# An encoder trunk in split fp32: FFN chunks and renewed residual turned by VectorE blocks and a bounce through HBM

## The reference

```
for layer in (0, 1):
    h = rms_norm(x, mixer_norm_w[layer])
    mixed = mixer(h) @ w_out          # layer 0: sliding-window attention and a gMLP gate; layer 1: stick-breaking attention
    x = x + mixed
    h = rms_norm(x, ffn_norm_w[layer])
    x = x + (silu(h @ w_gate) * (h @ w_up)) @ w_down    # hidden width 5632
```

## Time and profile before

| | |
|---|---|
| median of 3 runs | 2147.93 us (2147.77 to 2148.04) |
| the profiled execution | 2147.97 us, of which 2146.2 us is the span from first to last instruction |
| PE busy | 2136.4 us (100%) |
| DVE busy | 1196.3 us (56%) |
| ACT busy | 987.8 us (46%) |
| POOL busy | 8.8 us |
| DMA | 398.66 MB, 186 GB/s mean; the weights' queue took 55.7% of the 16 engines |

### The profile page before, as it was taken

The page is one execution under the profiler, slowest core; times in us unless marked ns, Lnnn a source line. Parts: engine busy times, 40 slices in busy tenths (PEclk is TensorE's granted clock), DMA queues, the critical chain, the costliest instruction groups (busy, mean ns, idle before and its releaser), DMA issues.

```text
span 2146.2 us, 26146 instructions
## 1 busy us (share of the span) xinstructions
PE 2136.4 (100%) x9708; PEld 1766.4 (82%) x9708; DVE 1196.3 (56%) x1314; ACT 987.8 (46%) x1150; POOL 8.8 (0%) x19
## 2 busy tenths in 40 slices
PE   9999999999999999999999999999999999999999
PEld 8777888888888888888888888888888888888887
DVE  6777555555555554555565566555555455554554
ACT  6466554443344434445455445554443444434443
POOL 1000000000000000000000000000000000000000
PEclk9999999999999999999999999999999999999999
DMA  9544565555556555545645554555555655556544
GB/s 327 189 138 150 183 196 189 183 196 185 196 188 194 183 192 195 194 158 189 200 160 159 174 176 157 178 194 196 178 193 195 196 179 194 191 190 191 192 157 157
DMA packets 199171, 398.66 MB, mean 186 GB/s; under 512 B 6640, under 2 KB 6656, under 8 KB 198848
## 3 DMA queue, kind: packets, MB, share of 16 engines
q1 hardware_dynamic: 197728, 392.72, 55.7%
q0 software_dynamic: 960, 2.90, 0.4%
q10 hardware_dynamic: 416, 2.13, 0.3%
HBM read 395.62 MB, written 2.10 MB: 185 GB/s over the span
## 4 chain that ended last, share of the span: by engine, by line
PE 98%; DVE 1%; ACT 1%; issue 0%; DMA 0%; DVEq 0%; SPq 0%
PE acc L980 31%; PE acc L982 31%; PE acc L981 31%; PE turn L996 2%; PE turn L1066 1%; PE turn L1116 0%; DVE w_lo L638 0%; PE zb L1091 0%; PE zb L1051 0%; ACT w_hi L434 0%; DMA raw<-in_w_in 0%; PE turn L1034 0%; PE turn L1117 0%; PE zb L1092 0%; ACT att L542 0%
## 5 line engine op out<-in xcount | busy, mean ns | idle before, releaser
L638 DVE TENSOR_TENSOR w_lo<-raw,w_hi 128x1024 fp32r<-128x1024 f32 (+1 forms) x760 | 905.2, 1201 | 647.2 <-ACT w_hi L434 645.5
L434 ACT ACTIVATE w_hi<-raw 128x1024 fp32r<-128x1024 f32 (+1 forms) x760 | 790.8, 1042 | 923.3 <-PE acc L982 920.4
L980 PE MATMUL acc<-w_hi,xT_hi 128*128 128x512 f32 x2016 | 793.3, 393 | 2.1 <-DVE w_lo L638 1.7
L982 PE MATMUL acc<-w_hi,xT_lo 128*128 128x512 f32 x2016 | 785.3, 390 | 0.0
L981 PE MATMUL acc<-w_lo,xT_hi 128*128 128x512 f32 x2016 | 785.0, 389 | 0.0
L980 PEld LDWEIGHTS acc<-w_hi,xT_hi 128*128 128x128 f32 x2016 | 378.7, 188 | 82.7 <-issue 6.0
L982 PEld LDWEIGHTS acc<-w_hi,xT_lo 128*128 128x128 f32 x2016 | 378.5, 188 | 79.0
L981 PEld LDWEIGHTS acc<-w_lo,xT_hi 128*128 128x128 f32 x2016 | 378.8, 188 | 78.2 <-issue 1.7
L980 PE MATMUL acc<-w_hi,m_hi 128*128 128x512 f32 x960 | 376.2, 392 | 1.8 <-DVE x_sb L725 0.9
L982 PE MATMUL acc<-w_hi,m_lo 128*128 128x512 f32 x960 | 373.8, 389 | 0.0
L981 PE MATMUL acc<-w_lo,m_hi 128*128 128x512 f32 x960 | 373.7, 389 | 0.0
(11 more groups left out here) (143 smaller groups left out, 547.2 us busy)
## 6 DMA issues: line engine op xcount, KB each, us to landing
raw<-in_w_gate SPq DMA_DIRECT2D x88, 1024.0 KB, 5.1
raw<-in_w_up SPq DMA_DIRECT2D x88, 1024.0 KB, 5.1
raw<-in_w_down SPq DMA_DIRECT2D x80, 1024.0 KB, 5.1
raw<-in_w_qkv SPq DMA_DIRECT2D x48, 1024.0 KB, 5.1
raw<-in_w_out SPq DMA_DIRECT2D x32, 1024.0 KB, 5.1
raw<-in_w_in SPq DMA_DIRECT2D x26, 1024.0 KB, 5.2
raw<-in_w_down SPq DMA_DIRECT2D x16, 512.0 KB, 3.7
raw<-in_w_in SPq DMA_DIRECT2D x4, 512.0 KB, 6.5
```

The source lines that it names most:

```text
L434: nc.scalar.activation(w_hi[:, s % RING, 0:nk, :], raw[:, u % RING, k:k + nk, :], ACTF.Copy).then_inc(hi_ready, 1)
L638: nc.vector.tensor_tensor(w_lo[:, s % RING, 0:nk, :], raw[:, (s // 2) % RING, k:k + nk, :], f32(w_hi[:, s % RING, 0:nk, :]), ALU.subtract) ...
L980: nc.tensor.matmul(dst, h, wh, start=q == 0 and k == 0, stop=False)
L982: ins = nc.tensor.matmul(dst, l, wh, start=False, stop=q == ph.per_chunk - 1 and k == nk - 1)
```

## The change

The eight TensorE transposes of each FFN chunk and of each renewed residual chunk go. In their place:

- DVE, right behind the last accumulator reading, transposes 32x32 blocks of the chunk into `folded` (`fold`, two instructions of 128x512).
- POOL writes `folded` (512 KB) to an HBM scratch `blocks` with one DMA, waits for it, and reads it back with four DMAs, one for each 32 partitions (128 KB each, runs of 512 bytes), into `spread` (`bounce`).
- ACT and DVE take from `spread` in place of `turn`, with the pieces of 32 positions put in order by their access patterns (`by_tile`), and at t = slots + 4 in place of slots + 1.
- PE waits for `fold_lo` in place of `dve_took`.

The turns of the layer's mixers (`in`, `qkv`) stay on PE. `qT` moves in the layout of SBUF, to give room to `folded` and `spread`. The diff's core:

```diff
+            def bounce(ph, i):
+                F = ph.fold(i)
+                pool.wait_ge(fold_done, F + 1)
+                pool.dma_start(blocks.rearrange("t p n -> p t n"), folded[:, :, :]).then_inc(fold_out, 16)
+                pool.wait_ge(fold_out, 16 * F + 16)
+                for b in range(QUARTERS):
+                    pool.dma_start(spread[b * BLK:(b + 1) * BLK, :, :, :].rearrange("j t a r -> j (t a) r"),
+                                   blocks[:, :, b * P:(b + 1) * P].rearrange("t (a j) r -> j (t a) r", a=QUARTERS)).then_inc(fold_landed, 16)
...
+            def fold_take_hi(ph, i, dst, src, scale=None):
+                act.wait_ge(fold_landed, 16 * QUARTERS * (ph.fold(i) + 1))
...
+                ins.then_inc(fold_hi, 1)
...
-                if t == ph.slots + 1:
-                    take_hi(ph.turn(i), [m_hi[:, bass.ds(4 * i, 4), :]], [turn[:, :].rearrange("p (k t) -> p k t", k=4)])
+                if t == ph.slots + 4:
+                    fold_take_hi(ph, i, [by_tile(m_hi[:, bass.ds(4 * i, 4), :])], [spread_tiles])
...
+            def fold(ph, i, src):
+                F = ph.fold(i)
+                dve.wait_ge(fold_out, 16 * F)
+                for tt in range(TT):
+                    ins = nc.vector.transpose(folded[:, tt, :].rearrange("p (b k t) -> p b k t", b=QUARTERS, k=GRP),
+                                              src[:, tt, :].rearrange("p (k b j) -> p b k j", k=GRP, b=QUARTERS))
+                ins.then_inc(fold_done, 1)
...
-                if t == 17:
-                    hv = m_hi[:, bass.ds(4 * i, 4), :]
-                    take_lo(ph.turn(i), [m_lo[:, bass.ds(4 * i, 4), :]], [turn[:, :].rearrange("p (k t) -> p k t", k=4)], [hv])
+                if t == ph.slots + 4:
+                    fold_take_lo(ph, i, [by_tile(m_lo[:, bass.ds(4 * i, 4), :])], [spread_tiles], [by_tile(m_hi[:, bass.ds(4 * i, 4), :])])
...
-                elif not prev.turns:
+                else:
+                    if prev.folds:
+                        pe.wait_ge(fold_lo, prev.fold((k0 + nk - 1) // 4) + 1)
                     return
-                else:
-                    K = prev.turn((k0 + nk - 1) // 4)
                 pe.wait_ge(dve_took, K + 1)
...
-            def up_work(ph, i, t):
-                if t == ph.slots + 1:
-                    pe.wait_ge(acc_read, 2 * ph.chunk(i, 1) + 2)
-                    turn_chunk(ph.turn(i), hid)
```

More of the change, by code:

```diff
@@ L46 @@
 GRP = CH // P
+BLK = 32
+QUARTERS = P // BLK
 FULL = [4] * (KT // 4)
@@ L66, with __init__ @@
 class Phase:
-    def __init__(self, n, unit0, chunk0, turn0, up0, before, rows0):
+    def __init__(self, n, unit0, chunk0, turn0, up0, before, rows0, fold0):
         self.name, self.count, self.chunks, self.unit_tiles, self.part = PHASES[n]
@@ L80, in __init__ @@
         self.unit0, self.half0, self.chunk0, self.turn0 = unit0, 2 * unit0, chunk0, turn0
-        self.turns = {"in": 23, "out": 1, "up": 1, "down": int(self.renews), "qkv": 4}[self.name]
+        self.turns = {"in": 23, "qkv": 4}.get(self.name, 0)
+        self.folds, self.fold0 = int(self.name == "up" or self.renews), fold0
     def half(self, i, s):
@@ L93, in turn, with fold @@
         return self.turn0 + i * self.turns + k
+    def fold(self, i):
+        return self.fold0 + i
     def tiles(self, s):
@@ L102, in make_phases @@
 def make_phases():
-    out, unit0, chunk0, turn0, up0, before, rows0 = [], 0, 0, 0, 0, 0, 0
+    out, unit0, chunk0, turn0, up0, before, rows0, fold0 = [], 0, 0, 0, 0, 0, 0, 0
     for n in range(len(PHASES)):
-        ph = Phase(n, unit0, chunk0, turn0, up0, before, rows0)
+        ph = Phase(n, unit0, chunk0, turn0, up0, before, rows0, fold0)
         out.append(ph)
@@ L110, in make_phases @@
         turn0 += ph.count * ph.turns
+        fold0 += ph.count * ph.folds
         up0 += ph.count if ph.name == "up" else 0
@@ L198, in build @@
         x_sb = sb("x_sb", [P, TT, D])
+        with ExitStack() as c0:
+            qT = sb("qT", [P, A_HEADS // 2, SEQ], F32, c0)
+        folded = sb("folded", [P, TT, CH])
+        spread = sb("spread", [P, TT, QUARTERS, P])
         raw = sb("raw", [P, RING, 4, CH])
@@ L279, in build @@
         x_added = sem("x_added")
+        fold_done, fold_out, fold_landed, fold_hi, fold_lo = (sem(n) for n in ("fold_done", "fold_out", "fold_landed", "fold_hi", "fold_lo"))
         kept = sem("kept")
@@ L382, in _ @@
                 pool.dma_start(dst, src).then_inc(small_landed, 16)
+            def bounce(ph, i):
[6 more added lines that the diff above has]
+                                   blocks[:, :, b * P:(b + 1) * P].rearrange("t (a j) r -> j (t a) r", a=QUARTERS)).then_inc(fold_landed, 16)
+            for ph in PH:
+                if ph.folds:
+                    for i in range(ph.count):
+                        bounce(ph, i)
             last = PH[-1]
@@ L464, in residual @@
                                              accum_out=squares[:, tt, bass.ds(i, 1)]).then_inc(squared, 1)
-                if t == ph.slots + 1:
-                    take_hi(ph.turn(i), [xT_hi[:, bass.ds(i * 4 + k, 1), :] for k in range(4)],
-                            [turn[:, k * SEQ:(k + 1) * SEQ] for k in range(4)],
-                            [normw_sb[:, row, bass.ds(i * 4 + k, 1)] for k in range(4)])
+                if t == ph.slots + 4:
+                    fold_take_hi(ph, i, [by_tile(xT_hi[:, bass.ds(i * 4 + k, 1), :]) for k in range(4)],
+                                 [spread_tiles[:, k:k + 1] for k in range(4)],
+                                 [normw_sb[:, row, bass.ds(i * 4 + k, 1)] for k in range(4)])
                 if t == ph.slots + 2:
@@ L681, in take_lo, with fold_take_lo @@
                 ins.then_inc(dve_took, 1)
+            def fold(ph, i, src):
[5 more added lines that the diff above has]
+                ins.then_inc(fold_done, 1)
+            def fold_take_lo(ph, i, dst, src, hi, scale=None):
+                dve.wait_ge(fold_hi, ph.fold(i) + 1)
+                for n, (d, s, h) in enumerate(zip(dst, src, hi)):
+                    if scale is None:
+                        ins = nc.vector.tensor_tensor(d, s, f32(h), ALU.subtract)
+                    else:
+                        ins = nc.vector.scalar_tensor_tensor(out=d, in0=s, scalar=scale[n], in1=f32(h), op0=ALU.mult, op1=ALU.subtract)
+                ins.then_inc(fold_lo, 1)
             def take(K, dst, src, scale=None):
@@ L710, in leave @@
                                                        in1=hid[:, tt, :], op0=ALU.mult, op1=ALU.mult).then_inc(acc_read, 1)
+                    dve.wait_ge(acc_read, 2 * ph.chunk(i, 1) + 2)
+                    fold(ph, i, hid)
                 else:
@@ L725, in leave @@
                         nc.vector.tensor_tensor(dst, acc[:, 0, tt, :], xs, ALU.add).then_inc(x_added, 1)
+                    if row is not None:
+                        dve.wait_ge(x_added, 2 * (before * (D // CH) + i) + 2)
+                        fold(ph, i, fresh(ph))
             def residual(ph, i, t):
@@ L730, in residual @@
                     return
[L731 to L735, removed]
+                if t == ph.slots + 4:
+                    fold_take_lo(ph, i, [by_tile(xT_lo[:, bass.ds(i * 4 + k, 1), :]) for k in range(4)],
+                                 [spread_tiles[:, k:k + 1] for k in range(4)],
+                                 [by_tile(xT_hi[:, bass.ds(i * 4 + k, 1), :]) for k in range(4)],
+                                 [normw_sb[:, row, bass.ds(i * 4 + k, 1)] for k in range(4)])
                 if isinstance(i, int) and i == ph.count - 1:
@@ L1001, in turn_chunk @@
                 turn_tiles(K, [(k * SEQ + tt * P, src[:, tt, k * P:(k + 1) * P]) for k in range(4) for tt in range(TT)])
[L1003 to L1007, removed]
             def in_work(t):
```

16 lines of the change are left out of this document (10 added, 6 removed).

## The result

| | before | after |
|---|---|---|
| median | 2147.98 us | 2176.38 us (2175.11 to 2177.37) |
| span of the profiled execution | 2146.2 us | 2173.2 us |
| PE busy | 2136.4 us | 2124.4 us |
| mean granted clock | 1.000 | 0.992 |

The account below looks back on a forecast made before the run. PE was taken to bound the kernel, with 98% of the chain. Saving 30.6 us less 11.5 us of waits gave -19.1 us, from 2147.97 to 2128.9, stated as 2129 us; range 2118 to 2163 us.

Parts of the forecast that it names:

- The saving, 34 x 0.90 = 30.6 us: On PE, eight transposes for each of 34 chunks go: 0.90 us a group, 30.6 us off the path.
- DVE's part: Two block transposes of 0.69 us each, done at T0 + 2.32; halves 2 and 3 move 1.38 us later, covered.
- T0: Start of the first matmul of the iteration after a chunk; the forecast counts the bounce's times from it.
- The write: POOL's 512 KB DMA to HBM: 3.1 us from issue to landing, in a load gap, landed at T0 + 5.7.
- The reads: POOL's four reads back, issued T0 + 6.0 to 8.2; near bounds 10.7 and 13.2, landing taken as T0 + 12.
- a load that gets between the reads: Rival: the queue serves only part of the reads before the next 1 MB load; L about 14, 2142 us, chance 0.17.
- L: Landing time of a bounce's last read, counted from T0; forecast at 12 us.
- The table of latest landings: Latest L without a PE stall for each kind of chunk, from 15.7 down to 8.5; at 12 only two kinds late.
- The clock: PE's granted clock: read as 1.00 while PE is never still; no case gave it a fall or a cost.
- 42 us of lateness: Within the rival of too long a bounce (chance 0.18): summed lateness of the chunks at L = 15, so 2159 us.
- The break-even: L = 14.4, where the summed lateness is about the 30.6 us saved; a longer bounce makes the kernel slower.
- 11.5 us: PE waits at L = 12: 7.0 for last up chunks before REST downs, 4.5 for renewed chunks in REST downs.

## Why the prediction was wrong, point by point

- **The saving, 34 x 0.90 = 30.6 us.** Right: 29.8 in the run without the bounce. The duration of 272 ns would have promised 74.
- **DVE's part.** Right: block transposes of 0.69 us, T0 + 2.3 forecast and 2.4 measured, and the delay of halves 2 and 3 hidden.
- **The write.** Right in the median: 3.2 us to landing against 3.1, in the gap of the earlier trace rows as said. In the renewing `down` it took 4.5 to 4.9 us for three of the four chunks.
- **The reads.** This is the step that failed. From the first issue I gave them 6 us, the middle of 2.5 and 5.0 for the last one. They took 9.1. The lower bound of 2.5 had no row behind it; with the loads held back it is 2.6 to 2.8. The upper one came from a constant at the start, and I had the right mechanism among the rivals, a load that gets between the reads, and priced it at L = 14 with a chance of 0.17. I spoke against it that all four reads are queued by T0 + 9. They are, but the load of half 3 was first in line, three of them passed behind it, and the fourth stood behind another load. The runs with loads a quarter as large (3.0 us less in layer 1) and with the load held back (4.6 us less) show it.
- **The table of latest landings.** Right in its order. At L = 15.3 it gives two waits of 6.8, three of 4.3 and 2.4 for the renewed chunks at a phase's end. Measured: 6.65 and 6.12; 3.7, 4.3 and 4.7; 2.2, 2.8 and none (a take at 11.6). The four `up` chunks before phases of 16 tiles were the exception: their takes came at 10.1 to 11.4 us and made no wait, where the table gives 1.4 each. The trace has one difference: there the next load is issued 0.3 us behind the fourth read, which lands in 4.6 to 5.9 us; at most other `up` chunks both are issued within 0.1 us of each other, and the read lands in 6.4 to 8.9. That fits the order of the queues; it isn't tested by a run of its own.
- **The clock.** Missing from every case. At L = 15 the text gave 42 us of lateness, so 2159 us; its own table adds up to 39 there, 41 with the half microseconds of the renewing `down`, and to 45 at 15.3. The waits were 39 us, and the four `up` chunks that were served sooner are about the difference. On top came matmuls at half clock: of the distances between the starts of neighbouring matmuls into `acc` with no wait between them, 66 lie above 0.34 us against 9 in the run without the bounce, and their excess over 0.2266 is 15.9 against 3.4 us, so 12.5. Some 6 us more of PE's busy time, against that run, I put down to refilling the pipeline after fifteen waits, which is argued and not shown. The sum against that run, from the spans: 56.6 = 37.8 standing + 18.8 busy, and 18.8 = 12.5 + 6.3. So the forecast had 11.5 us for what came to 56.6: the waits, which the late reads made, and a slow clock that it put at nothing.
- **The break-even.** Forecast at L = 14.4, without the clock. The four wide reads, with the take at 10.2 and so L = 12.6, gave 2149.5, as long as before. With the clock's part and the REST phases' larger lateness (takes of 10.6 to 12.9 there, against a median of 10.2) it lies 1.8 us earlier.

## What to carry to other kernels

A latency can replace work on the bound engine only as far as each consumer's due time allows, and the tightest consumers (here 5 of 34 chunks made 26 of 39 us of waiting) settle the sign. Before sending a latency-critical DMA through a busy memory system, ask which bulk transfers stand ahead of each of its pieces and put it ahead of them in the same queue: the same five DMAs gave 2124 us ahead of a load and 2212 us behind it. A small read among 1 MB loads can wait for more than one of them: here the loads cost the four reads 4.6 us of 12.9, part of it before the first read and part before the fourth.

## What was not expected of the hardware

- The granted clock fell from 1.00 to 0.50 in or right behind all five waits of PE of 3.7 us and more, and the matmuls behind them ran at a distance of 0.43 us in place of 0.2266. With filling matmuls in place of a wait of 6 us it stayed at 1.00. The shorter waits don't sort by length. Behind one of 2.06 us, which ends at 1408.61, the clock fell too (the windows below), behind one of 2.8 us at 1452 it stayed at 1.00, and the run with SP's bounce behind the load has both kinds too, a fall with a wait of 2.7 us (at 307) and none with one of 2.8 (at 237). Which of them lose the clock no run here settles.

```profile
1406.00:1408.00 2.00, 0.55 (x3) 0.12 (x1) 2.00 (x5) 2.00 (x3) 0.00 (x0) 1.00 0.00 0
1408.00:1410.00 2.00, 1.39 (x4) 1.15 (x5) 2.00 (x3) 1.26 (x2) 0.00 (x0) 0.73 0.11 15
1410.00:1412.00 2.00, 2.00 (x7) 1.52 (x6) 1.38 (x2) 0.00 (x0) 0.00 (x0) 0.50 0.85 295
```

- Among the loads of weights, four reads into 32 partitions each, in runs of 512 bytes, made the take 2.7 us later than four into 128 partitions in runs of 1 KB, same bytes and same number. With the loads held back the narrow ones landed 2.6 to 2.8 us after issue, so they are slow in company, not by themselves; whether the width or the runs do it isn't shown.
- A write of 512 KB to HBM and four reads of it back take 6.9 us from the first issue when nothing stands ahead of them in SP's queue, and 7.9 in POOL's with the loads held back, on a kernel that moves 205 GB/s in the mean.
